# First block's input transposed on the host and used un-normalised, its roots applied at evictions; first loads in pieces; three pieces of side work moved

## The reference

```python
h = rms_norm(x, norm1_g)                 # x * rsqrt(mean(x*x)) * g, per token
proj = h @ w_in
(rx, rgate, q, kc, vc, ks, vs, kw, vw, nsa_g, mg_rnn, mg_attn) = split(proj)
hr = rg_lru(causal_dwconv(rx, ...), ..., lru_lambda)     # gated recurrence
o = nsa(rms_norm(q per head), compress(kc), compress(vc), rms_norm(ks), vs, rms_norm(kw), vw, nsa_g, ...)
x = x + (sigmoid(mg_rnn) * (hr * gelu(rgate)) @ w_rnn_out + sigmoid(mg_attn) * o @ w_attn_out) @ w_out
x = x + ffn(x)                           # and then the second block: mixer, layer norm, SwiGLU, layer norm
```

## Time and profile before

| | us |
|---|---|
| runs (3) | 812.19 to 812.41, median 812.38 |
| span of the profiled execution | 810.6 |
| its own time | not given apart; the median of the runs is 1.8 above the span |
| TensorE busy | 799.6 |
| VectorE, ScalarE, GpSimd busy | 599.4, 487.0, 27.1 |

### The profile page before, as it was taken

How to read it: one execution, slowest core, us unless ns; L and a number is a source line. 1 busy time by engine, 2 the same in 40 slices (tenths; PEclk the granted TensorE clock), 3 DMA queues, 4 the chain that set the end, 5 groups by cost and what they waited for, 6 DMA issues and landing times.

```text
span 810.6 us, 11913 instructions
## 1 busy us (share of the span) xinstructions
PE 799.6 (99%) x4813; PEld 693.2 (86%) x4813; DVE 599.4 (74%) x773; ACT 487.0 (60%) x738; POOL 27.1 (3%) x38
## 2 busy tenths in 40 slices
PE   8999999999999999999999999999999999999996
PEld 7889998888888888988888888888888988888885
DVE  6774698998957986897878778877777665655556
ACT  6555598877757454765666566546755654544552
POOL 1102000000000000000000000020110000000000
PEclk9999999999999999999999999999999999999999
DMA  8446432342434674456455555764453655555441
GB/s 337 164 156 251 170 126 104 118 155 73 151 119 159 229 288 156 156 188 227 160 206 174 201 197 175 256 237 147 146 196 121 211 201 196 174 219 191 161 152 52
DMA packets 22630, 143.79 MB, mean 177 GB/s; under 512 B 2608, under 2 KB 3248, under 8 KB 8240
## 3 DMA queue, kind: packets, MB, share of 16 engines
q1 hardware_dynamic: 20880, 137.72, 48.3%
q10 hardware_dynamic: 1696, 5.31, 1.8%
HBM read 141.97 MB, written 1.05 MB: 176 GB/s over the span
## 4 chain that ended last, share of the span: by engine, by line
PE 93%; ACT 3%; DVE 2%; DMA 1%; issue 1%; DVEq 0%; SPq 0%; ACTq 0%
PE PS L1748 19%; PE PS L1752 10%; PE PS L1801 10%; PE PS L1802 10%; PE PS L1805 10%; PE PS L1735 5%; PE PS L1736 4%; PE PS L1740 4%; PE PS L2115 3%; PE PS L1764 2%; PE PS L2094 2%; PE PS L1858 1%; PE PS L1892 1%; PE PS L2119 1%; PE PS L1869 1%; PE PS L2065 1%
## 5 line engine op out<-in xcount | busy, mean ns | idle before, releaser
L1074 DVE TENSOR_TENSOR WL<-RAW,WH 128x2048 fp32r<-128x2048 f32 (+2 forms) x127 | 285.1, 2247 | 31.1 <-ACT WH L629 31.0
L629 ACT ACTIVATE WH<-RAW 128x2048 fp32r<-128x2048 f32 (+2 forms) x127 | 238.2, 1877 | 47.0 <-PE PS L1805 25.7
L1490 DVE TENSOR_TENSOR HLS<-PS,HLS 128x512 f32<-128x512 f32 x46 | 31.7, 689 | 92.7 <-ACT HLS L977 92.7
L1748 PE MATMUL PS<-CHL,WH 128*128 128x512 f32 x352 | 87.9, 392 | 0.0
L1735 PE MATMUL PS<-BHL,WH 128*126 128x256 f32 (+1 forms) x336 | 83.6, 287 | 0.0
L977 ACT ACTIVATE HLS<-PS 128x512 f32<-128x512 f32 x46 | 27.4, 595 | 90.7 <-PE PS L1752 86.3
L1736 PE MATMUL PS<-BHL,WH 128*126 128x256 f32 (+1 forms) x336 | 81.8, 282 | 0.0
L1748 PE MATMUL PS<-BHL,WH 128*128 128x512 f32 x320 | 79.9, 392 | 0.0
L1748 PEld LDWEIGHTS PS<-CHL,WH 128*128 128x128 f32 x352 | 63.9, 189 | 11.8
L1802 PE MATMUL PS<-WH,AHL 128*128 128x512 f32 x176 | 68.8, 391 | 0.0
L1801 PE MATMUL PS<-WH,AHL 128*128 128x512 f32 x176 | 68.7, 390 | 0.0
(11 more groups left out here) (313 smaller groups left out, 1311.1 us busy)
## 6 DMA issues: line engine op xcount, KB each, us to landing
RAW<-in_w_stream SPq DMA_DIRECT2D x108, 1024.0 KB, 4.8
RAW<-in_w_stream SPq DMA_DIRECT2D x11, 1008.0 KB, 4.9
RAW<-in_w_stream SPq DMA_DIRECT2D x8, 704.0 KB, 4.5
WF<-in_w_stream SPq DMA_DIRECT2D x2, 1024.0 KB, 5.4
LN<-in_ln ACTq DMA_DIRECT2D x2, 1024.0 KB, 5.2
WF<-in_w_stream SPq DMA_DIRECT2D x4, 294.0 KB, 3.6
X<-in_x SPq DMA_DIRECT2D x2, 512.0 KB, 4.2
RAW<-in_w_stream SPq DMA_DIRECT2D x2, 512.0 KB, 6.8
```

The lines of the kernel that those rows point to most:

```text
L629: eng.activation(WH[:, c % NSLOT, 0:CHUNKS[c][2]], raw(c), ACT.Copy).then_inc(w_hi, 1)
L1074: eng.tensor_tensor(WL[:, c % NSLOT, 0:CHUNKS[c][2]], raw(c), f32(WH[:, c % NSLOT, 0:CHUNKS[c][2]]), ALU.subtract).then_inc(w_lo, 1)
L1490: eng.tensor_tensor(HLS[:, n % 4, :, :], PS[:, bank:bank + 2, 0:TOK], HLS[:, n % 4, :, :], ALU.add)\
L1748: eng.matmul(PS[:, bank, :], wh, HL[:, k, :, :].rearrange("p a t -> p (a t)"), start=(k == 0), stop=False)
```

## The change

1. The host also passes `x` transposed (`xt`, with `norm1_g` in front, 128 x (8 + 8 x 256)). It is loaded in two halves, the first on ScalarE's queue. `CH`, `CL` are made from it times `norm1_g`, without the root. `kv` and `q` chunks use `CH`, `CL`; there are no transposes at the start, and 11 fills.
2. Chunks 0 and 1 are loaded in halves and cut, and multiplied, in slices of 512 columns (one slice of 128 rows `k`).
3. The order of chunks is `kv` x4, `q` x2, `cmp` x2, `q` x2, `w1` x2. `x` itself, the constants and the columns are loaded behind chunk 3.
4. The roots: squares at chunk 1; a matmul of ones against the diagonals of roots behind `kv` 3 gives the roots along the free dimension; VectorE multiplies the transposed input by it and by `norm1_g` (8 products, `input_normed`), ScalarE and VectorE cut this into `BH`, `BL` for `cmp` and all later chunks. Token-major results are scaled at their evictions; GpSimd multiplies `krs` and `rq` by the root.
5. The decay chain stands at chunk `W0` (`decay_rates`), the scaling of the second query half at the two `w1` chunks (`queries_normed(1, i)`), in each case behind VectorE's `split`; key scaling one or two chunks after the sums.
6. Semaphores of the two feed-forward parts are merged; nothing of their order changes.

```diff
@@ chunk_list
     out = [("kv", i, CHUNK, True) for i in range(4)]
+    out += [("q", i, CHUNK, True) for i in range(2)]
     out += [("cmp", i, CHUNK, True) for i in range(2)]
-    out += [("q", i, CHUNK, True) for i in range(4)]
+    out += [("q", i, CHUNK, True) for i in range(2, 4)]
@@ sync
-            for t in range(NT):
-                eng.dma_start(X0[:, t, :], A_x[t * P:(t + 1) * P, :]).then_inc(x_in[t], 16)
             for c in LOAD_ORDER:
-                if c == 2:
-                    eng.dma_start(CN[:, P:NCONST], A_consts[:, P:NCONST]).then_inc(const_in, 16)
+                if c == 4:
+                    for t in range(NT):
+                        eng.dma_start(X0[:, t, :], A_x[t * P:(t + 1) * P, :]).then_inc(x_in[t], 16)
+                    eng.dma_start(CN[:, :], A_consts).then_inc(const_in, 16)
                     eng.dma_start(CV[:, :], A_cols).then_inc(const_in, 16)
...
                     if c == 0:
-                        eng.dma_start(raw(c)[:, first], source[:, first]).then_inc(w0_in, 16)
-                        eng.dma_start(raw(c)[:, second], source[:, second]).then_inc(raw_in[slot], 16)
+                        eng.dma_start(raw(c)[:, 0:1024], source[:, 0:1024]).then_inc(w0_in, 16)
+                        eng.dma_start(raw(c)[:, 1024:CHUNK], source[:, 1024:CHUNK]).then_inc(raw_in[slot], 16)
+                        rest = slice(KD + 4 * TOK, KD + KD * TOK)
+                        eng.dma_start(XTG[:, rest], A_xt[:, rest]).then_inc(xt_in[1], 16)
+                    elif c == 1:
+                        eng.dma_start(raw(c)[:, 0:1024], source[:, 0:1024]).then_inc(w1_in, 16)
+                        eng.dma_start(raw(c)[:, 1024:CHUNK], source[:, 1024:CHUNK]).then_inc(raw_in[slot], 16)
@@ gpsimd: the keys' roots, and alike the queries'
-                power(krs[:, 8 * b:8 * b + 8], kss[:, 8 * b:8 * b + 8], 8, HD, EPS, k_rstd)
+                power(krs[:, 8 * b:8 * b + 8], kss[:, 8 * b:8 * b + 8], 8, HD, EPS)
+                for t in range(NT):
+                    h = slice(8 * b + 4 * t, 8 * b + 4 * t + 4)
+                    eng.tensor_scalar(krs[:, h], krs[:, h], rsx[:, t:t + 1], None, ALU.mult).then_inc(k_rstd, 1)
@@ scalar
+            eng.dma_start(XTG[:, 0:KD + 4 * TOK], A_xt[:, 0:KD + 4 * TOK]).then_inc(xt_in[0], 16)
+            first_high(0, w0_in)
+            first_high(1, w0_in)
+            gained_hi(1)
...
+                if kind == "q" and i == 0:
+                    for kp in range(4):
+                        eng.wait_ge(xt_ready, 1 + kp + 1)
+                        eng.activation(BH[:, 2 * kp:2 * kp + 2, :], XT[:, 2 * kp:2 * kp + 2, :], ACT.Copy).then_inc(xt_hi, 1)
@@ vector
+            def x_squares():
+                for t in range(NT):
+                    eng.wait_ge(x_in[t], 16)
+                    eng.scalar_tensor_tensor(XN[:, t, 512:DM], X0[:, t, 512:DM], 1.0 / DM, X0[:, t, 512:DM], ALU.mult, ALU.mult,
+                                             accum_out=ssx[:, 2 * t + 1:2 * t + 2]).then_inc(x_sq2, 1)
+            def roots_diagonal():
+                eng.wait_ge(const_in, 32)
+                for t in range(NT):
+                    eng.wait_ge(x_rstd, t + 1)
+                    eng.tensor_scalar(DG[:, t, :], ident, rsx[:, t:t + 1], None, ALU.mult).then_inc(dg_ready, 1)
+            def input_normed():
+                eng.wait_ge(chunk_done, AT["kv", 3] + 1)
+                for k in range(KD):
+                    ins = eng.scalar_tensor_tensor(XT[:, k, :], XT[:, k, :], XTG[:, k:k + 1], PS[:, RS_BANK, 0:TOK],
+                                                   ALU.mult, ALU.mult)
...
+                if c == 1:
+                    x_squares()
+                    roots_diagonal()
                 if CHUNKS[c][:2] not in SUMS_FIRST and kind != "ri" and c != W0 and c + 1 != UNIT_FIRST or c == SPLIT_AHEAD:
                     split(c + 2)
...
+                if c == 3:
+                    input_normed()
+                    keys_normed(0)
...
+                if kind == "w1":
+                    queries_normed(1, i)
+                if c == W0:
+                    decay_rates()
                 side(c)
@@ tensor
+                    if i == 3:
+                        eng.wait_ge(dg_ready, NT)
+                        for t in range(NT):
+                            last = eng.matmul(PS[:, RS_BANK, P * t:P * t + P], WARM[:, :], DG[:, t, :], start=True, stop=True)
```

More of the change, by code:

```diff
@@ L574, in power @@
                 link(eng.tensor_scalar(t, ss, 1.0 / mean_of, eps, ALU.mult, ALU.add))
-                eng.tensor_tensor(out, t, half[0:out.shape[0], 0:n], ALU.pow).then_inc(ready, 1)
+                ins = eng.tensor_tensor(out, t, half[0:out.shape[0], 0:n], ALU.pow)
+                if ready is None:
+                    link(ins)
+                else:
+                    ins.then_inc(ready, 1)
             link(eng.memset(half[:, :], -0.5))
@@ L1012, in gained_hi @@
[L1012 to L1019, removed]
-            eng.dma_start(CN[:, 0:P], A_consts[:, 0:P]).then_inc(g1_in, 16)
-            for t in range(NT):
-                eng.wait_ge(x_in[t], 16)
-                eng.activation(XN[:, t, 0:512], X0[:, t, 0:512], ACT.Square, scale=DM ** -0.5,
-                               accum_out=ssx[:, 2 * t:2 * t + 1]).then_inc(x_sq, 1)
@@ L1033, in _, with gained_hi, first_high @@
-            split(1)
+                eng.activation(AH[:, i % NA, :], SG[:, i % 4, :], ACT.Copy).then_inc(up_hi, 1)
+            def gained_hi(k):
+                eng.wait_ge(xt_in[k // 4], 16)
+                eng.activation(CH[:, k, :], XT[:, k, :], ACT.Copy, scale=XTG[:, k:k + 1]).then_inc(xt_hi, 1)
+            def first_high(k, arrived):
+                eng.wait_ge(arrived, 16)
+                part = slice(512 * (k % 4), 512 * (k % 4) + 512)
+                eng.activation(WH[:, k // 4, part], raw(k // 4)[:, part], ACT.Copy)\
+                   .then_inc(w_hi if k % 4 == 3 else w_part_hi, 1)
@@ L1703, in _ @@
                     rg_scan(G)
+                if c == 3:
+                    input_normed()
+                    keys_normed(0)
+                if c == 4:
+                    for kp in range(4):
+                        eng.wait_ge(xt_hi, KD - 1 + kp + 1)
+                        pair = slice(2 * kp, 2 * kp + 2)
+                        eng.tensor_tensor(BL[:, pair, :], XT[:, pair, :], f32(BH[:, pair, :]), ALU.subtract).then_inc(xt_lo, 1)
+                if c == 5:
+                    keys_normed(1)
+                if kind == "w1":
+                    queries_normed(1, i)
+                if c == W0:
+                    decay_rates()
                 side(c)
@@ L1728, in transposes, with f_tile @@
                             last.then_inc(done, 1)
-            def f_tile(out, c, col0, m, H, L, nk=KD, parts=P):
+            def f_tile(out, c, col0, m, H, L, nk=KD, parts=P, first_use=False):
                 s = c % NSLOT
@@ L2152, in main @@
                 if kind in ("dn", "dn2"):
-                    first_bank, lo_s, n_all = (2, up_lo, N_UP // 2) if kind == "dn" else (0, up2_lo, N_UP2 // 2)
+                    first_bank, before, n_all = (2, 0, N_UP // 2) if kind == "dn" else (0, N_UP, N_UP2 // 2)
                     def down_half(cc, j, t, n):
@@ L2171, in main @@
                         eng.wait_ge(w_hi, SPLIT_NO[c + 1] + 1)
-                        eng.wait_ge(lo_s, 2 * i + 3)
-                        eng.wait_ge(up_hi if kind == "dn" else up2_hi, 2 * i + 4)
+                        eng.wait_ge(up_lo, before + 2 * i + 3)
+                        eng.wait_ge(up_hi, before + 2 * i + 4)
                         s = (c + 1) % NSLOT
```

283 lines of the change are left out of this document (147 added, 136 removed).

## The result

The changed kernel takes **818.01 us** (median of 4 runs, 816.98 to 818.55) against 812.31 (4 runs, 812.19 to 812.41): ratio 1.0068, 95% interval 1.0056 to 1.0080. It is slower, by more than the forecast (813.1) and beyond the range (811.0 to 815.0).

The account below looks back on a forecast made before the run. TensorE, busy 799.6 of 810.6 us, bounds the kernel. Terms -3.5 + 0.25 - 0.1 + 0.47 + 3.6 = +0.7 give 811.3; with the 1.8 between median and span, 813.1, range 811.0 to 815.0.

Parts of the forecast that it names:

- the late middle: Rival, chunk 3 and BH copies: loads 1.5 us or more late use up the cover; some +1.5, 814.6; chance 0.10.
- First matmul: Start: without transposes, both first loads land at 5.9 and the first weight matmul starts at 6.65, 3.5 us earlier.
- my upper bound of 6.6: Start: first loads land at 6.6 if the second half megabyte takes 2.17 us; gain then 2.8.
- The lower bound: Start: each first load lands at 4.46 as tile 0 did alone; fills still run to 5.4; gain 4.8.
- Chunks 0 and 1: Same 48 matmuls; a wait of 0.25 us for VectorE's first cut, less 0.1 for a shorter first group.
- Roots as a matmul: Behind the fourth kv chunk: two fp32 128x128 matmuls of ones against the diagonals, 0.47 us on the path.
- Decay chain: 17 VectorE instructions, 46.68 to 49.78 in the old trace: hidden before and staying hidden, no cost.
- Roots, now late: Chunks 1 to 8: VectorE's later roots, cuts and low copies stay covered, costed at nothing; cover 1.1 us.
- the two places with 1.1 of cover: Low part of chunk 3 (done 23.9, wanted 25.0) and last low copy (done 40.3, wanted 1.4 after 40.0).
- Late query evictions: First rnn tile: both second-half evictions stand behind low parts on VectorE; 3.6 us of new wait, bounds 3.2 to 3.8.
- Clock loss: Rival, behind the new rnn wait: clock falls to 1.2 GHz, 1.7 us more lost, 814.8; chance 0.14.
- The sum: Whole kernel: -3.5 + 0.25 - 0.1 + 0.47 + 3.6 = +0.7 us, forecast 813.1; bounds 811.4 to 814.0.

Follow-up runs that it names:

- experiment 10: Kernel before the change, with only the decay chain moved from the second cmp chunk to chunk W0: 812.26 us, ratio 1.0000.
- experiment 4: Changed kernel with the third raw buffer also open to the first two q chunks: 816.59 us, ratio 1.0049.
- experiment 5: Changed kernel with the two diagonals of roots placed behind the cut of chunk 3, no buffer added: 815.18 us, ratio 1.0037.
- experiment 1: Changed kernel with the second query half's scalings ahead of VectorE's cut in each w1 chunk: 813.52 us, ratio 1.0014.
- experiment 2: Kernel before the change, with only the second query half's two scalings moved behind VectorE's cuts in the w1 chunks: 817.39 us, ratio 1.0063.
- experiment 3: Changed kernel with 30 fill matmuls, results unread, on TensorE ahead of the wait at the first rnn tile: 815.79 us, ratio 1.0042.
- experiment 6: Changed kernel with second-query-half scalings ahead of the cuts and the third raw buffer open to the first two q chunks: 811.40 us, ratio 0.9993.
- experiment 7: Kernel of experiment 6 with GpSimd's product of rq and root taken into the root, one operation less: 811.17 us, ratio 0.9987.
- experiment 8: Kernel of experiment 6 with 13 fills at the start in place of 11: 811.35 us, ratio 0.9989.
- experiment 9: Changed kernel with the edits of experiments 1, 4, 7 and 8 together: 810.96 us, ratio 0.9985.

## Why the prediction was wrong

Right in the start and in the wait at the `rnn` chunk, wrong in the total by 4.9 us: a result within 0.2% of the kernel before had 0.68, and it is 0.7% slower. **Two terms that the sum put at nothing failed: the late middle (measured 1.9) and the clock behind the new wait (measured 1.4 to 1.5 in the profile).** Both had been named as rivals, and their signs, idle time released by `BHL` and slow matmuls behind the wait, both came.

- *First matmul*: forecast 6.65 and a gain of 3.5; measured 7.11 and 3.06. The copy began at 6.40, 0.5 later than the landing that I took, still inside my upper bound of 6.6. Two half megabytes on two queues did not land together as soon as the same 1 MB in one queue (5.99); no run shows why. The lower bound was wrong too: the 11 fills ran to 6.16, not 5.4, so no landing could have brought the first matmul to 5.4 in this execution. **Mis-sized by 0.44.**
- *Chunks 0 and 1*: 0.15 forecast, 0.29 measured. *Roots as a matmul*: 0.47, and 0.47 to 0.5. *Decay chain*: nothing, and nothing (experiment 10).
- *Roots, now late*: **the step that failed by its reasoning.** "The low part of chunk 5 lands by its load (26.2)" took the loads as a stream of 2.5 us per MB. A load starts when its buffer is free, and the buffer of chunk 5 was freed by the low part of chunk 3 at 25.24, which itself stood behind the second diagonal. The load landed at 29.92, 3.7 later than written; 1.1 of cover, some 0.5 by which TensorE was itself later, and about 1.9 of new idle took it up. Of the two places with 1.1 of cover, chunk 3 held (its low part was done at 25.2, forecast 23.9) and the low copies did not. Experiments 4 and 5 each remove the cause in a different way, and each takes the wait away.
- *Late query evictions*: 3.6 forecast, 3.5 measured, and the cause is settled by moving them (experiments 1 and 2). This working by the order of three engines was the sound part.
- *Clock loss*: I gave it 0.14, since no row showed a fall. The case came, and its size, 1.7 by the fills' rate, was near (1.4 in the profiled run, 1.7 in experiment 4, 2.2 to 2.5 between medians in experiment 3). **The chance was wrong.** That the size fits is in part luck, as the fills' slow time is not the same in every execution: the 14 fills that took 5.02 before took 6.34 in experiment 2. And one reading behind it was wrong. The mean clock of 0.998 was taken as the slow start and nothing else, but the stretches of TensorE in the kernel before say:

```profile
0.00:6.10 6.10, 5.00 (x28) 1.00 0.65 228
806.00:810.60 4.60, 0.00 (x0) 0.57 0.46 171
```

The low clock that the mean contains lies in the last 4.6 us, behind TensorE's last matmul (0.43 x 4.6 = 2.0 us, which is 0.0024 of the span). TensorE had been idle since 803.4. So a fall of the clock behind idle time did stand in the trace, at its very end. An idle stretch of 1.35 that does not lower the clock says nothing for one of 3.6, and the new idle was longer than any in the trace between two matmuls. In the profiles the clock fell behind all four idle stretches of 3.4 to 3.5 (the change, experiments 2, 4 and 5), for 3.4 us each, and behind none of the shorter ones (up to 1.6 at the `cmp` and `rnn` chunks). The Trainium skill (TensorE: Matmul & The Clock Gate, HAM oscillation) says that waits of a few microseconds between groups of matmuls bring the half rate back; the trace of the change and experiment 2 agree with it, 0.50 behind 3.5 and 3.4 us of idle.
- *The sum*: with the late middle (1.9), the clock (1.5) and the smaller start (0.4) the forecast of 813.1 becomes 816.9; the profiled run took 816.98, the median is 818.01. Both rivals came at once. I had priced each alone (814.8 and 814.6), so that the range ended at 815.0, although nothing in them excludes each other: the one is at 42 us, the other at 75.

## What to carry to other kernels

For every transfer that is moved in the order, find first what frees its buffer, and on which engine that instruction stands behind what: the issue time comes from this, the queue's rate only bounds it. An edit that leaves TensorE idle for longer than the trace has yet shown without a fall of the clock has to be costed with the slow matmuls behind it (here 1.4 to 1.7 us in the profiles on 3.5 of wait), and two independent rivals have to be added, not put side by side. An eviction that frees a PSUM bank belongs ahead of a cut that nobody waits for yet; here two such instructions of 0.68 us cost 4.5.

## What the runs showed that was not expected

A small operation of GpSimd, which takes 0.20 us elsewhere in the same kernel, took 4.58:

```profile
39.26 4.58 POOL L594 TENSOR_SCALAR tmp<-kss 128x8 f32<-128x8 f32 x1 [9.83 <-DVE kss L1307]
68.89 0.20 POOL L594 TENSOR_SCALAR tmp<-qss 128x8 f32<-128x8 f32 x1
```

It began at 39.26, inside VectorE's cut of chunk 6, and ended at 43.84, just after the last of the four subtractions that follow the cut without a gap (43.78, the rows of the middle above). Likewise line 619 took 0.31 at 68.49 and 0.85 at 70.92, where it ended 0.17 behind the cut that ran beside it (71.60). The Trainium skill (SBUF — State Buffer, Who interferes with whom) says that VectorE, reading two SBUF operands, and GpSimd reading SBUF exclude each other, and that the one that comes second waits. The rows agree, and show a GpSimd operation held through five VectorE instructions; it took the same 4.58 in the profiles of all eight other kernels with this order. Nobody waited for this one. Line 619 is different: in experiments 1 and 6 it took 0.95 and 1.40 beside the cut of chunk 12, and VectorE's second eviction waited 0.21 for it. Experiment 7, which takes the operation away, gained 0.2.

The number of fills goes with the spread between runs. With 11 fills, 4 of 11 runs of experiment 6 and 2 of 11 of experiment 7 were 1 to 2 us slower than the rest (and 1 of 11 of experiment 1); with 13 fills, in experiments 8 and 9, none of 22 was. The counts speak for the two more fills. What happens in the slower runs is open: no profile of one was taken, and their mean clocks (0.995, 0.995, 0.997 and 0.999 in experiment 6, where the faster runs have 0.997 and 0.998) do not tell them apart.
